# The second norm's root and shift applied behind the router's products, which take the rows without them

## What is computed

```
h2   = rms_norm(x, norm2_g) * (1 + scale2) + shift2        # x = x + gate1 * (merged @ w_out)
aff  = softmax(h2 @ w_router)                               # 16 experts, float32
gate, idx = top_k(swapaxes(aff), 2 * L / 16)                # each expert picks its tokens
xs   = h2[idx]
hid  = silu(xs @ w_gate[e]) * (xs @ w_up[e])                # EXPERT_FF = 2816
out  = (hid @ w_down[e]) * gate;   x += gate2 * scatter_add(out);   y = rms_norm(x, final_norm_g)
```

## Time and profile before

| | us |
|---|---|
| median of 3 runs | 1967.24 (1966.66 to 1969.98) |
| the profiled execution's own time | 1968.58 |
| its span | 1966.8 |
| PE busy | 1896.0 (96%) |
| DVE busy | 1199.5 (61%) |
| ACT busy | 394.4 (20%) |
| POOL busy | 407.8 (21%) |
| on the chain that ended last | PE 56%, DMA 28%, DVE 9% |

### The profile page before, as it was taken

The page is one execution under the profiler, slowest core; times in us unless marked ns, Lnnn a source line. Parts: engine busy times, 40 slices in busy tenths (PEclk is TensorE's granted clock), DMA queues, the critical chain, the costliest instruction groups (busy, mean ns, idle before and its releaser), DMA issues.

```text
span 1966.8 us, 64418 instructions
## 1 busy us (share of the span) xinstructions
PE 1896.0 (96%) x28661; PEld 1423.3 (72%) x28661; DVE 1199.5 (61%) x1976; ACT 394.4 (20%) x909; POOL 407.8 (21%) x406
## 2 busy tenths in 40 slices
PE   8999999999998999999999999999999999999996
PEld 5888899999884788788878566655556565556663
DVE  3532441231556767777677776767777676777674
ACT  4332332222331112111121111111111121111113
POOL 3032009100412130220311213031120302113021
PEclk8999999999999999999999999999999999999998
DMA  8244532212389999999999999999999999999997
GB/s 338 85 158 159 177 114 80 90 50 86 122 346 351 413 406 419 407 411 415 407 417 411 412 414 407 419 407 411 416 412 414 407 419 408 411 415 412 415 410 300
DMA packets 150464, 647.59 MB, mean 329 GB/s; under 512 B 11420, under 2 KB 56344, under 8 KB 134024
## 3 DMA queue, kind: packets, MB, share of 16 engines
q1 hardware_dynamic: 134576, 617.71, 78.3%
q0 software_dynamic: 15648, 29.02, 5.1%
q10 hardware_dynamic: 184, 0.06, 0.0%
HBM read 632.47 MB, written 14.40 MB: 329 GB/s over the span
## 4 chain that ended last, share of the span: by engine, by line
PE 56%; DMA 28%; DVE 9%; issue 3%; SPq 2%; ACT 1%; POOL 1%; POOLq 0%; DVEq 0%; ACTq 0%
DMA ring<-in_w_exp_gate_dram 25%; PE bank L2064 16%; PE bank L2493 12%; PE bank L2521 7%; PE bank L2510 6%; DVE sums L1790 4%; PE bank L2503 4%; PE bank L2185 3%; PE bank L2332 3%; SPq L584 2%; DVE hid_t L1855 2%; DMA ring<-in_w_exp_down_dram 1%; PE bank L2418 1%; PE bank L2035 1%; PE bank L2046 1%
## 5 line engine op out<-in xcount | busy, mean ns | idle before, releaser
L1790 DVE TENSOR_TENSOR sums<-ring 128x704 f32<-128x704 f32 x744 | 609.4, 885 | 249.7 <-DMA ring<-in_w_exp_gate_dram 209.2
L2493 PE MATMUL bank<-ring,hid_t 128*32 128x256 f32 x8184 | 473.5, 384 | 34.1 <-DVE hid_t L1862 33.4
L2521 PE MATMUL bank<-ring,xs_t 128*32 128x352 f32 x5952 | 448.0, 459 | 0.2 <-issue 0.2
L2493 PEld LDWEIGHTS bank<-ring,hid_t 128*32 128x32 f32 x8184 | 282.2, 111 | 198.5 <-DVE hid_t L1862 40.4
L2521 PEld LDWEIGHTS bank<-ring,xs_t 128*32 128x32 f32 x5952 | 248.7, 110 | 184.8 <-issue 123.3
L2510 PE MATMUL bank<-sums,xu_a 128*32 128x176 f32 x5952 | 252.9, 313 | 0.2 <-issue 0.2
L2510 PEld LDWEIGHTS bank<-sums,xu_a 128*32 128x32 f32 x5952 | 208.6, 110 | 18.6 <-issue 0.6
L847 POOL TENSOR_TENSOR small<-kpow 128x2 f32<-128x2 f32 x31 | 13.3, 428 | 968.4 <-DVE out_rows L1923 806.2
L1224 ACT ACTIVATE v_both<-bank 128x176 f32<-128x176 f32 x31 | 9.8, 317 | 843.5 <-PE bank L2510 843.5
L2064 PE MATMUL bank<-act_hi,wt_hi 128*128 128x320 f32 x448 | 138.8, 310 | 0.8 <-DVE rtmp L1582 0.8
L1332 DVE TENSOR_TENSOR wt_lo<-raw_t,wt_hi 128x2048 fp32r<-128x2048 f32 x25 | 57.5, 2301 | 134.4 <-ACT wt_hi L944 134.4
(11 more groups left out here) (389 smaller groups left out, 2351.6 us busy)
## 6 DMA issues: line engine op xcount, KB each, us to landing
ring<-in_w_exp_gate_dram SPq DMA_DIRECT2D x127, 1408.0 KB, 25.2
ring<-in_w_exp_up_dram SPq DMA_DIRECT2D x127, 1408.0 KB, 27.7
ring<-in_w_exp_down_dram SPq DMA_DIRECT2D x96, 1536.0 KB, 25.8
ring<-in_w_exp_down_dram SPq DMA_DIRECT2D x32, 1024.0 KB, 30.1
raw_t<-in_w_ada_dram SPq DMA_DIRECT2D x16, 1024.0 KB, 5.3
raw_t<-in_w_in_dram SPq DMA_DIRECT2D x14, 1024.0 KB, 5.1
a_raw<-in_w_ada_dram SPq DMA_DIRECT2D x8, 1024.0 KB, 16.8
raw_t<-in_w_branch_gate_dram SPq DMA_DIRECT2D x8, 1024.0 KB, 5.4
```

Source lines behind the costliest of these rows:

```text
L1790: nc.vector.tensor_tensor(sums[:, (N_SUM * i + j) % SUM_SLOTS], w[:, k, :, n, :], w[:, kk, :, nn, :], ALU.add if sign > 0 else ALU.subtrac ...
L2493: ins = mm(bank[5 + x // 2][c * Q:(c + 1) * Q, x % 2 * DC:(x % 2 + 1) * DC], hid_t[:, f, x * Q:(x + 1) * Q], w[:, j, c * DC:(c + 1) * DC], ...
L2521: ins = mm(bank[UP_BANK[x]][c * Q:(c + 1) * Q, 0:FC], xs_t[:, x, k * Q:(k + 1) * Q], w[:, kk, c * FC:(c + 1) * FC], start=k == 0, stop=k = ...
```

## The change

The router's logits are linear in `h2`: h2 @ w = inverse root * ((x * gs2) @ w) + shift @ w. The new kernel uses this.

- VectorE's `second_norm(i)` becomes `scaled` (x2 times `gs2`, no root, counted by `s_u`), `inverse_root` and `shifted` (in place: times the inverse root, plus `sh2`, counted by `s_h2`). `shifted` waits for `tr_full`, since TensorE transposes the scaled rows that it overwrites.
- TensorE's `h2_transpose(i)` waits for `s_u`, and `router(i)` for each half of ScalarE's copies. The logits get root and shift in `logits(i)` on VectorE, from the bank into `aff`.
- The shift's part, two rows of 16 (`sw`), is made once: `shift_rows` and `shift_spread` on TensorE, two copies on ScalarE between weight splits, a memset and two copies on VectorE.
- For the last tile the steps are interleaved: scaling inside `residual(4)`, `h2_to_t` in halves around `norm_root(4)`, `router(3)` behind the first half of the last transposes. The fillers `keep_warm(11, 7)` and `keep_warm(4, 7)` are gone. `e_used` 6 now comes at the first product of `prompt_spread`. `h2_transpose(1)` stands ahead of `router(0)`.

```diff
-            def second_norm(i):
+            def scaled(i, c):
+                lt = ORDER[i]
+                cs = slice(c * 512, (c + 1) * 512)
+                if i >= 2 and c == 0:
+                    dve.wait_ge(s_h2w[ORDER[i - 2]], 16)
+                    dve.wait_ge(tr_full, TR.full(("h2", ORDER[i - 2], 1)))
+                dve.wait_ge(s_x2, 2 * i + c + 1)
+                nc.vector.tensor_tensor(h2[:, i % 2, cs], x2[:, X2_POS[lt], cs], gs2_b[int(lt == NS)][:, cs], ALU.mult)\
+                  .then_inc(s_u, 1)
+            def inverse_root(i):
+                lt = ORDER[i]
+                dve.wait_ge(s_sqrt, NT + i + 1)
+                tick(nc.vector.reciprocal(small[:, 24 + lt:25 + lt], small[:, 16 + lt:17 + lt]))
+            def shifted(i):
...
                 for c in range(2):
                     cs = slice(c * 512, (c + 1) * 512)
-                    tick(nc.vector.scalar_tensor_tensor(out=h2[:, i % 2, cs], in0=x2[:, X2_POS[lt], cs],
-                                                        scalar=small[:, 24 + lt:25 + lt], in1=gs2_b[cnd][:, cs],
-                                                        op0=ALU.mult, op1=ALU.mult))
-                    nc.vector.tensor_tensor(h2[:, i % 2, cs], h2[:, i % 2, cs], sh2_b[cnd][:, cs], ALU.add).then_inc(s_h2, 1)
+                    dve.wait_ge(tr_full, TR.full(("h2", lt, c)))
+                    nc.vector.scalar_tensor_tensor(out=h2[:, i % 2, cs], in0=h2[:, i % 2, cs],
+                                                   scalar=small[:, 24 + lt:25 + lt], in1=sh2_b[cnd][:, cs],
+                                                   op0=ALU.mult, op1=ALU.add).then_inc(s_h2, 1)
+            def second_norm(i):
+                for c in range(2):
+                    scaled(i, c)
+                inverse_root(i)
+                shifted(i)
+            def logits(i):
+                lt = ORDER[i]
+                dve.wait_ge(s_lg, i + 1)
+                tick(nc.vector.scalar_tensor_tensor(out=aff[:, lt, :], in0=bank[LG_BANK[lt]][:, lt * NE:(lt + 1) * NE],
+                                                    scalar=small[:, 24 + lt:25 + lt], in1=sw[:, int(lt == NS), :],
+                                                    op0=ALU.mult, op1=ALU.add))
...
             residual(4)
             prompt_lists()
-            second_norm(4)
+            inverse_root(4)
+            dve.wait_ge(s_lg, 4)
+            for i in range(1, 4):
+                logits(i)
+            shifted(4)
+            logits(4)
             softmax(1, 0, NS)
+            prompt_gates()
...
+            def shift_rows():
+                o = tr(("sw", 0, 0))
+                pe.wait_ge(s_const, 16 * N_CONST)
+                for k in range(KT):
+                    ins = mm(o[0:2, 0:NE], ada_t[:, 3 * KT + k, :], wr_sb[:, k, :], start=k == 0, stop=k == KT - 1)
+                ins.then_inc(tr_full, 1)
...
             wo_chunk(3, 0)
+            h2_transpose(1)
             pe.wait_ge(wo_read, 6)
             router(0)
-            h2_transpose(1)
             wo_chunk(3, 1)
```

78 lines of the change are left out of this document (48 added, 30 removed).

## The result

| | before | after |
|---|---|---|
| median of the runs | 1966.95 us (4 runs, 1966.49 to 1969.98) | 1980.21 us (4 runs, 1976.94 to 1982.35) |
| ratio | | 1.0060, 95% interval 1.0048 to 1.0073 |
| profiled execution, its span | 1968.58, 1966.8 | 1982.35, 1980.5 |
| mean granted clock | 0.988 | 0.981 |

The kernel became slower by 13 us; 5.4 were forecast and the range ended at 1975.2. In the expert stage the two traces do the same: share of the DMA engines 1.02, 411 GB/s against 412, and from the issue of the first sample gather to the end of the span 1357.6 us against 1357.0. So the time is lost ahead of that gather, where the forecast looked for it.

What follows compares the result with a forecast made beforehand. The expert stage was taken to run at its weight stream's rate, so only delays ahead of it count: first sample gather +3.7 us plus one clock drop +1.7 gives +5.4, a median of 1972.6 us, range 1968.3 to 1975.2.

Steps and rivals of the forecast that it cites:

- both holes of the stream: Gaps in the weight stream at 560 to 580 (6.4 us) and 600 to 620 (4.4 us), before the expert stage.
- Shift rows: Added small products shift_rows and shift_spread on TensorE, mostly hidden in its wait for the weight split: 0.3 us in all.
- first stand: TensorE idle ahead of router(0), waiting for residual(2), which VectorE now starts behind shifted(1): 3.0 us.
- The clock: TensorE's granted clock drops to 1.2 GHz after an idle wait; one such drop taken, at 1.7 us.
- second stand: TensorE idle ahead of the prompt's small transpose, waiting for the prompt's softmax, now behind shifted(2): 2.3 us of delay.
- a rival with 0.16: Both new idle waits of TensorE are followed by the lower clock: +7.1 us, 1974.3; chance 0.16.
- The end of the stage: From TensorE's last product on, the lists' softmax comes 4.3 us earlier and h2 0.9 earlier.
- the lists' feeder: VectorE's index lists ahead of the first sample gather; prompt gather landing in 2.9 to 7.9 us, lists at 612.5.
- the other feeder: GpSimd's gate loads behind the last h2 store, ahead of the sample gather; store landing 12.7 us, ready at 613.5.
- no gain at the end: Router's last products bound by the root, softmax keeping its old distance: +5.6 us, 1972.8; chance 0.05.
- Store against stream: Last h2 store waits behind weight pieces queued before it, 12.7 us; rival of queues taking turns: 1968.5, chance 0.08.
- Stands covered: Rival: residual(2) keeps its place, TensorE never idles, gather 2.0 to 3.0 us earlier, 1964.7; chance 0.13.

Runs made afterwards that it cites:

- both_moved: Changed kernel with residual(2) moved ahead of shifted(1) and the prompt's softmax ahead of second_norm(2) on VectorE; ratio 1.0027 to the kernel before.
- after_again: The changed kernel run again, unchanged, on the chip of the experiments; ratio 1.0059 to the kernel before.
- warm_fit: Changed kernel with 13 and 10 idle products of 128 columns filling TensorE's two new waits; ratio 1.1598 to the kernel before, its expert loop stalled.
- warm_half: Changed kernel with 26 and 20 idle products of 64 columns in TensorE's two new waits; ratio 1.0043 to the kernel before.
- before_late7: Kernel before with one early weight load, lone7, issued as late as in the changed kernel; ratio 0.9999 to the kernel before.
- last_only: Kernel before with only tile 4 taking root and shift behind the products, shift-row products included; ratio 0.9998 to the kernel before.
- last_only_2: Second run of the kernel with only tile 4 in the new way; ratio 1.0005 to the kernel before.
- last_x2w: Only tile 4 in the new way, and the first three x2 stores wait for x2 instead of h2; ratio 1.0007 to the kernel before.
- last_best: Only tile 4 new, x2 stores freed, two top-list rounds ahead of the prompt gather's wait, 32 short idle pairs on TensorE; ratio 1.0005 to the kernel before.

## Why the prediction was wrong

*What bounds the kernel.* Right: nothing changed behind the first gather, and both holes of the stream moved with TensorE's marks.

*Shift rows, and the new wait on VectorE.* Right to 0.1 us each: 0.3, a first stand of 3.1 for 3.0, a second of 2.4 for 2.3. both_moved shows that the two orders on VectorE are their cause: without them TensorE comes to its last product as before.

*The clock.* This is the step that failed most. The forecast took one fall at 1.7 us; there were two, and they cost 4.7 and 2.5, 5.5 us more than it had (3.6 and 2.4 in after_again; warm_fit and warm_half give 5.8 to 7.0 for both). The number was wrong by its source: the 1.7 was what one block of 72 products lost in the expert loop, and what a fall costs goes by how long it lasts and what work stands in it, here a router tile and most of 24 products of 512 columns. 8.9 us from 563.08 at the clock of 0.50 lose 4.5 at half speed, the rows say 4.7; 5.9 us from 580.08 lose 3.0, the rows say 2.7 with the small transpose. The Trainium skill ("TensorE: Matmul & The Clock Gate", section "Terms") has this as a rule: the penalty is the time at the reduced clock times the missing share. This trace agrees. That the second stand brings a second fall stood in the forecast as a rival with 0.16. It deserved more: the wait in the rows that came nearest in length, the one before 607.1, had its fall, and nothing set the second stand apart from the first. It was not certain either, as the block at 1253.71 and the fall of before_late7 show.

*The end of the stage.* The mechanism was right up to the softmax (4.1 us nearer to the last product, 4.3 forecast), and the gain ended there: the forecast's -1.9 came out at +0.3. The step that failed is the lists' feeder: the prompt gather was given 2.9 to 7.9 us to land, the middle taken. It took 7.8 in last_only and 8.9 in after, and VectorE waits for it ahead of the top list. The 7.9 "at most" of the kernel before was no bound: in after GpSimd's queue still carried the stores of the tile before, issued at 592.84 and 593.37, the second of which landed after 14.7 us, at 608.1; in the kernel before it took 7.6 us and had landed 2.5 us ahead of the gather's issue. Nor would a faster gather have won the 1.9, for the other feeder was mis-sized too: the last store landed after 13.71 us, forecast 12.7, and the gate loads ended 25.15 us behind the last product, forecast 23.8. The rival "no gain at the end" had 0.05.

*Store against stream.* From its row of 11.41 us the forecast concluded that a store waits behind the pieces queued before it, and that the trace speaks against the rule by which the queues take turns, packet by packet (the Trainium skill, "DMA: Bandwidth & Descriptors", section "Queues, rings and completion order"). That reading was wrong. The packets, MB and share of the stream's queue (q1) and of GpSimd's (q0), first at 596 to 598 in the kernel before, then at 598 to 600 in the changed one:

```profile
q1 hardware_dynamic: 93, 0.52, 62.9%
q0 software_dynamic: 94, 0.32, 39.2%
```
```profile
q1 hardware_dynamic: 48, 0.59, 75.7%
q0 software_dynamic: 49, 0.20, 24.3%
```

Packet for packet the two queues take turns, and in the changed kernel they do so from 598 to 614 (85 and 85 at 608 to 610, 99 and 98 at 612 to 614): the trace agrees with the rule. What was wrong is "half the rate". The stream's packets were the larger ones, 12 KB against 4 KB at 598 to 600, so GpSimd's queue got a quarter of the bytes there, and about two fifths in the other window. In the kernel before, moreover, GpSimd's queue moved only 0.13 MB between the store's issue and 594, as much as the prompt gather has (128x256 f32), so the store's own bytes seem to begin some 3 us after its issue; the forecast allowed 1.8 for start and end together. So its 6.9 us was the right rule with a wrong share and a wrong start. 17 further last `h2` stores took 10.7 to 12.0 us where tiles 0 to 3 were in the old way and 12.3 to 14.0 in the others.

*Rivals.* "Stands covered" is both_moved. The forecast gave it -2.5 us; it is +5.3. The gain at the end is missing (the gather goes out 25.8 and 25.6 us behind the last product, before 25.7), and the rest no part of the forecast names: 3.0 us on the gather's landing and 1.5 to 2.7 on the first expert's products. Some 2 us of that went when the `x2` stores no longer waited for `h2`. In the changed kernel itself it doesn't show (landing 2.80, products 19.18): there `lone3` goes out 10.5 us later than before, but the last product comes 12.6 later.

What stays open: the traces of last_only_2, last_x2w and last_best sum to 0.1 to 1.7 us below the kernel before (the 0.3 of the shift rows, ahead of the first transposes, not counted), and their ratios lie 1.0 to 1.4 us above it. Their intervals are 2 us wide to either side, so it can't be told whether something ahead of the first transposes costs them 1 to 3 us or nothing does.

## What to carry to other kernels

An operation that overwrites its input in place must wait for the last reader, and since the engine runs its instructions in the order written, that wait falls on everything queued behind it: put the next tile's work, above all what frees a bank, ahead of it. Price a stand of TensorE as the stand plus half of the time at the lower clock behind it, and look at what work stands there, not at what a fall cost elsewhere. A gain at the end of a stage counts only as far as the next wait in that engine's queue; find it, and the fillings that were cut to the old gaps, before booking the gain. Two DMA queues that both have work shared the engines by packets here, so ask for the size of the packets before giving a store half of the rate.
